# One factor and one shift for the first layer norm with modulation, the first head's scores earlier, gathers ahead of low parts, late weights in 8 KB rows

## The reference

```python
def ada_mod(c, w, b):
    m = jax.nn.silu(c) @ w + b
    shift, scale, gate = jnp.split(m, 3, axis=-1)
    return shift[:, None, :], 1.0 + scale[:, None, :], 1.0 + gate[:, None, :]

def layer_norm(x, g, b):
    xf = x.astype(jnp.float32)
    mu = jnp.mean(xf, axis=-1, keepdims=True)
    var = jnp.mean(jnp.square(xf - mu), axis=-1, keepdims=True)
    return ((xf - mu) * lax.rsqrt(var + LN_EPS)).astype(x.dtype) * g + b

def chunk(xc):                       # in peer_ffn, 128 tokens at a time
    q = (xc @ w_q).reshape(PEER_CHUNK, PEER_HEADS, 2, PEER_HALF)
    s = jnp.einsum('thpd,pnd->thpn', q, sub_keys).astype(jnp.float32)
    sv, si = lax.top_k(s, PEER_TOPK)
    ...
    top_s, pos = lax.top_k(cand_s, PEER_TOPK)
    idx = jnp.take_along_axis(cand_i, pos, axis=-1)
    g = jax.nn.softmax(top_s, axis=-1).astype(xc.dtype)
    act = jax.nn.gelu(jnp.einsum('td,thkd->thk', xc, u[idx]), approximate=False)
    return jnp.einsum('thk,thkd->td', g * act, v[idx])

def second_block(x, c, ...):
    for i in range(DEPTH):           # DEPTH = 2: short convolution, then differential attention
        shift, scale, gate = ada_mod(c, ada_w[i, 0], ada_b[i, 0])
        h = x * scale + shift
        f = mixer(h)
        x = layer_norm(DEEPNORM_ALPHA * x + gate * f, ln_g[i, 0], ln_b[i, 0])
        shift, scale, gate = ada_mod(c, ada_w[i, 1], ada_b[i, 1])
        h = x * scale + shift
        f = peer_ffn(h, peer_w_q[i], peer_sub_keys[i], peer_u[i], peer_v[i])
        x = layer_norm(DEEPNORM_ALPHA * x + gate * f, ln_g[i, 1], ln_b[i, 1])
    return x
```

## Time and profile before

| | |
|---|---|
| median of three runs | 2437.72 us (2437.59 to 2440.14) |
| the profiled execution | 2435.66 us, its span 2433.8 us |
| TensorE | busy 2106.9 us, 87% |
| VectorE | busy 1599.6 us, 66% |
| ScalarE | busy 1138.1 us, 47% |
| GpSimd | busy 639.6 us, 26% |
| DMA | 768.23 MB, mean 316 GB/s |
| the chain that ended last | PE 51%, DMA 25%, DVE 11%, ACT 8% |

### The profile page before, as it was taken

How to read it: one execution, slowest core, us unless ns; L and a number is a source line. 1 busy time by engine, 2 the same in 40 slices (tenths; PEclk the granted TensorE clock), 3 DMA queues, 4 the chain that set the end, 5 groups by cost and what they waited for, 6 DMA issues and landing times.

```text
span 2433.8 us, 28455 instructions
## 1 busy us (share of the span) xinstructions
PE 2106.9 (87%) x9804; PEld 1352.1 (56%) x9804; DVE 1599.6 (66%) x3701; ACT 1138.1 (47%) x2760; POOL 639.6 (26%) x624
## 2 busy tenths in 40 slices
PE   7769999998999987897777989987998898888776
PEld 7648999876999986452223434432444443323222
DVE  5685677664778777867667467556648656676753
ACT  4354543534653434435445375434447444444543
POOL 0010011000001004544443234243324334434441
PEclk8869999999999988999999999999999999999998
DMA  6234588541569745999999999999999999999995
GB/s 226 87 104 147 174 280 283 173 165 41 171 215 361 268 148 190 396 419 419 419 420 407 392 412 413 395 418 420 395 389 369 398 381 420 420 420 420 420 421 212
DMA packets 139013, 768.23 MB, mean 316 GB/s; under 512 B 15232, under 2 KB 18048, under 8 KB 73088
## 3 DMA queue, kind: packets, MB, share of 16 engines
q0 software_dynamic: 87552, 587.24, 59.6%
q1 hardware_dynamic: 50608, 177.81, 20.7%
q10 hardware_dynamic: 720, 1.51, 0.2%
HBM read 765.45 MB, written 1.05 MB: 315 GB/s over the span
## 4 chain that ended last, share of the span: by engine, by line
PE 51%; DMA 25%; DVE 11%; ACT 8%; issue 3%; POOL 1%; SPq 0%; ACTq 0%; POOLq 0%; DVEq 0%
DMA arena<-experts,arena 24%; PE bank L860 12%; PE bank L513 9%; PE bank L515 9%; PE bank L514 9%; PE bank L895 6%; DVE arena L2120 3%; DMA wring<-w_stream 2%; ACT L1335 1%; ACT arena L1340 1%; ACT arena L1339 1%; ACT arena L1157 1%; DVE arena L1678 1%; PE bank L613 1%; DVE wlo L1566 1%
## 5 line engine op out<-in xcount | busy, mean ns | idle before, releaser
L860 PE MATMUL bank<-arena 128*128 128x512 f32 x2048 | 983.2, 618 | 168.0 <-ACT arena L1340 167.6
L2120 DVE CUSTOM_DVE_ANT_0 arena<-arena 128x1024 f32<-128x1024 f32 x512 | 631.2, 1234 | 468.4 <-DMA arena<-experts,arena 467.4
L480 POOL DMA_INDIRECT arena<-experts,arena x512 | 560.0, 1094 | 862.6 <-PE bank L860 820.2
L860 PEld LDWEIGHTS bank<-arena 128*128 128x128 f32 x2048 | 374.1, 194 | 730.3 <-ACT arena L1340 374.8
L1566 DVE TENSOR_TENSOR wlo<-wring,whi 128x1024 fp32r<-128x1024 f32 x224 | 272.9, 1224 | 168.1 <-ACT whi L1083 167.3
L1083 ACT CAST whi<-wring 128x1024 fp32r<-128x1024 f32 x236 | 246.3, 1048 | 275.4 <-PE bank L515 274.0
L1335 ACT ACTIVATE arena<-arena 128x1 f32<-128x1 f32 x512 | 102.9, 201 | 472.3 <-DVE arena L2120 470.5
L1340 ACT ACTIVATE arena<-tab,arena 128x128 f32<-128x128 f32 x512 | 205.5, 401 | 16.7
L513 PE MATMUL bank<-hTh,whi 128*128 128x256 f32 (+1 forms) x640 | 192.3, 300 | 22.0 <-DVE hTl L1575 18.9
L466 POOL DMA_DIRECT2D arena<-ada_w x64 | 34.0, 531 | 664.7 <-DVE adaM L1613 646.5
L514 PE MATMUL bank<-hTl,whi 128*128 128x256 f32 (+1 forms) x640 | 187.3, 293 | 0.0
(11 more groups left out here) (304 smaller groups left out, 3039.1 us busy)
## 6 DMA issues: line engine op xcount, KB each, us to landing
wring<-w_stream SPq DMA_DIRECT2D x332, 512.0 KB, 4.7
arena<-ada_w POOLq DMA_DIRECT2D x64, 512.0 KB, 5.3
alibi<-ada_w POOLq DMA_DIRECT2D x32, 512.0 KB, 5.4
arena<-experts,arena POOLq DMA_INDIRECT x512, 14.2
xT<-xT_in SPq DMA_DIRECT2D x1, 1088.0 KB, 5.0
alibi<-alibi_in ACTq DMA_DIRECT2D x1, 1024.0 KB, 5.0
outT<-xT SPq DMA_DIRECT2D x2, 512.0 KB, 13.5
tab<-tab_in SPq DMA_DIRECT2D x1, 831.0 KB, 6.5
```

The lines of the kernel that those rows point to most:

```text
L480: pool.indirect_dma_start(g_ring[:, r], None, experts[n // (2 * PEER_HEADS)], bass.IndirectOffsetOnAxis(idx[:, s // SLOTS % 2, s % SLOTS:s ...
L860: last = mm(banks[2 * t + b][:, :], diag[:, r], g_ring[:, r, D + b * TILE_N:D + (b + 1) * TILE_N], start=s % SLOTS == 0, stop=s % SLOTS == ...
L2120: v.tensor_tensor_reduce(g_ring[:, r, 0:D], g_ring[:, r, 0:D], hrow[:, t], 1.0, 0.0, ALU.mult, ALU.add, act8[:, r:r + 1]).then_inc(dot_don ...
```

## The change

- The first layer norm with its modulation becomes one factor and one shift: `hf` is first the normalized value times g x (1 + scale); ScalarE adds the folded shift as the bias of the operation that makes `hTh`, VectorE's low part adds it too. The shift is added to `hf` itself afterwards (`hf_ready`), and the plain layer norm `x2` after that (`ln_done`). Three small products on VectorE before the residual make factor and shift.
- TensorE makes the first head's scores right behind its own two query chunks; scores of later heads stand between the two chunks of the next head. ScalarE copies in the same order.
- GpSimd does four low parts, waits for `ln_done`, and then issues gathers, with the low parts of tile 57 after slots 1, 2, 4 and 6; its wait for the turned rows stands at slot 3.
- The late 24 tiles come as two DMAs of 1 MB each, with rows of 8 KB; the host lays them out so that a half holds the rows of four steps of the contraction, and `half_tile` waits for and frees a half.
- The fifteen partial products leave the first attention: three go into the first MLP's start, twelve into the section of keys, values and queries of the second attention.

```diff
-        both_g, both_b = m(2, KC), m(2, KC)
+        both_g, both_b = m(3, KC), m(3, KC)
...
+        late_landed = [[sem(f"late_landed{s}_{h}") for h in range(2)] for s in range(2)]
...
+        def late_half(g, half):
+
+            return wring[:, g % 2, 2 * half:2 * half + 2].rearrange("p c k n -> p (c k n)")
...
-            for g in range(N_LOADS):
+            for g in range(G_QKV):
...
-                    sp.dma_start(wring[:, g % 2, c], w_stream[g if g < N_TILES else g - BESIDE, c]).then_inc(w_landed[g % 2][c], 16)
+                    sp.dma_start(wring[:, g % 2, c], w_stream[g, c]).then_inc(w_landed[g % 2][c], 16)
...
+            for g in range(G_QKV, N_LOADS):
+                tile = w_stream[g if g < N_TILES else g - BESIDE].rearrange("c p k n -> (c p k n)").rearrange(
+                    "(h p m) -> h p m", h=2, p=P)
+                for half in range(2):
+                    sp.wait_ge(lin_done, CPT * (g - 2) + 2 * half + 2)
+                    sp.dma_start(late_half(g, half), tile[half]).then_inc(late_landed[g % 2][half], 16)
...
             for c in range(CPT):
                 split_lo(G_PQ + 1, c)
-            split_lo(G_PQ + 2, 0)
-            pool.wait_ge(hrow_done, 4)
+            pool.wait_ge(ln_done, 8)
             for s in range(N_SLOTS):
+                if s == 3:
+                    pool.wait_ge(hrow_done, 4)
                 gather(s)
-                if s in (1, 3, 5):
-                    split_lo(G_PQ + 2, (s + 1) // 2)
+                if s in (1, 2, 4, 6):
+                    split_lo(G_PQ + 2, s // 2)
...
-                if half == 0:
-                    for c in range(CPT):
-                        pe.wait_ge(w_landed[g % 2][c], 16 * (g // 2 + 1))
-                for kc in range(4 * half, 4 * half + 4):
-                    last = mm(dst, lhs[:, kc], wring[:, g % 2, :, kc], start=kc == 0, stop=kc == KC - 1)
-                if half:
-                    last.then_inc(lin_done, CPT)
+                pe.wait_ge(late_landed[g % 2][half], 16 * ((g - G_QKV) // 2 + 1))
+                w = late_half(g, half)
+                for k in range(4):
+                    last = mm(dst, lhs[:, 4 * half + k], w[:, k * TILE_N:(k + 1) * TILE_N], start=half == 0 and k == 0,
+                              stop=half == 1 and k == 3)
+                last.then_inc(lin_done, CPT // 2)
...
+            def query_chunk(c):
+                if c >= 4:
+                    pe.wait_ge(pq_copied, c - 3)
+                chunk(G_PQ + c // CPT, c % CPT, banks[(2, 3, 6, 7)[c % 4]][:, 0:SEQ], pq_in, after(mod_split, 8) if c == 0 else None)
...
             for h in range(PEER_HEADS + 1):
                 if h < PEER_HEADS:
-
-                    for c in (2 * h, 2 * h + 1):
-                        g = G_PQ + c // CPT
-                        if c >= 4:
-                            pe.wait_ge(pq_copied, c - 3)
-                        chunk(g, c % CPT, banks[(2, 3, 6, 7)[c % 4]][:, 0:SEQ], pq_in, after(mod_split, 8) if c == 0 else None)
-                if h:
-
-                    y = h - 1
-                    if y == 0:
-                        pe.wait_ge(sk_landed, 16)
-                    pe.wait_ge(pq_copied, 2 * y + 2)
-                    if y >= 2:
-                        pe.wait_ge(sc_copied, y - 1)
-                    for t in range(2):
-                        for x in range(2):
-                            last = mm(banks[4 + y % 2][:, (2 * t + x) * P:(2 * t + x + 1) * P],
-                                      pqT[:, y % 2, x, t * P:(t + 1) * P], skT[:, x], start=True, stop=True)
-                    last.then_inc(sk_done, 1)
+                    query_chunk(2 * h)
...
+                if h >= 2:
+                    head_scores(h - 1)
+                if h < PEER_HEADS:
+                    query_chunk(2 * h + 1)
+                if h == 0:
+                    head_scores(0)
                 if 1 <= h < 3:
                     t = h - 1
                     for c in range(KC):
+                        if t == 0:
+                            pe.wait_ge(hf_ready, c + 1)
...
-            act.wait_ge(ln_done, 1)
+            act.wait_ge(mod_ready, 9)
...
-            hi_parts(hTh, hf, 0, SEQ, mod_ready, mod_hi, 8)
+            for kc in range(KC):
+                act.wait_ge(mod_ready, 8 + kc + 1)
+                af(hTh[:, kc, 0:SEQ], hf[:, kc], ACT.Identity, bias=both_b[:, 0, kc:kc + 1]).then_inc(mod_hi, 1)
...
-                    for x in range(2):
-                        c = 2 * h + x
-                        act.wait_ge(lin_done, CPT * G_PQ + c + 1)
-                        nc.scalar.copy(pqT[:, h % 2, x], banks[(2, 3, 6, 7)[c % 4]][:, 0:SEQ]).then_inc(pq_copied, 1)
-                        if c < 12:
-                            split_hi(G_PQ + c // CPT + 1, c % CPT)
-                if h:
-                    y = h - 1
-                    act.wait_ge(sk_done, y + 1)
-                    nc.scalar.copy(sc[:, y], banks[4 + y % 2][:, :].rearrange("p (t s n) -> p t s n", t=2, s=2)).then_inc(
-                        sc_copied, 1)
+                    query_copy(2 * h)
+                if h >= 2:
+                    copy_scores(h - 1)
+                if h < PEER_HEADS:
+                    query_copy(2 * h + 1)
+                if h == 0:
+                    copy_scores(0)
+                if 2 * h + 1 < 12:
+                    query_hi(2 * h + 1)
...
-                parts = ((0, 0, 0, 0, 1, 1, 1, 2, 2, 2, 2, 1, 1, 1, 1), (0, 0, 0, 0, 0, 0, 0, 0, 0, 0, 0))[layer]
...
-                    for _ in range(parts[n]):
-                        ada_part()
...
-                two(0, 1, True)
+                two(0, 1, True, 0 if layer else 3)
...
-                if x % 2:
-                    ada_part()
+                ada_part()
             for x in range(8):
                 split_lo(G_BQ + x // CPT + 1, x % CPT)
                 if x == 0:
                     head_root(0)
-                if x % 2:
-                    ada_part()
+                ada_part()
                 if x >= 2:
                     head_scale(x - 2)
             head_scale(6)
@@ -1902,12 +1934,14 @@
             split_lo(G_BV + 1, 1)
             for x in range(3):
                 head_scale(8 + x)
+                ada_part()
             decay_sums()
             split_lo(G_BV + 1, 2)
             split_lo(G_BV + 1, 3)
             for x in range(3, 6):
                 head_scale(8 + x)
                 ada_part()
+            ada_part()
...
+            def first_layer_norm():
...
+                for n in range(KC + 2):
+                    if n < KC:
+                        v.scalar_tensor_tensor(hf[:, n], xnT[:, n], both_g[:, 0, n:n + 1], rinv[:, 0, 0:SEQ], ALU.mult,
+                                               ALU.mult).then_inc(mod_ready, 1)
+                    if n >= 2:
+                        c = n - 2
+                        dve.wait_ge(mod_hi, 8 + c + 1)
+                        v.scalar_tensor_tensor(hTl[:, c, 0:SEQ], hf[:, c], both_b[:, 0, c:c + 1], hTh[:, c, 0:SEQ].bitcast(F32),
+                                               ALU.add, ALU.subtract).then_inc(mod_split, 1)
+                for c in range(KC):
+                    v.tensor_scalar(hf[:, c], hf[:, c], both_b[:, 0, c:c + 1], None, ALU.add).then_inc(hf_ready, 1)
                 scaled = []
-                for n in range(KC + 4):
+                for n in range(KC + 1):
                     if n < KC:
-                        mark(v.scalar_tensor_tensor(xnT[:, n], xnT[:, n], vcol("ln_g", 8 * i + n), rinv[:, 0, 0:SEQ], ALU.mult,
-                                                    ALU.mult))
+                        mark(v.scalar_tensor_tensor(xnT[:, n], xnT[:, n], vcol("ln_g", n), rinv[:, 0, 0:SEQ], ALU.mult, ALU.mult))
                         scaled.append(seq[0])
-                    if 1 <= n < KC + 1:
-                        c = n - 1
-                        dve.wait_ge(dve_seq, scaled[c])
-                        v.tensor_scalar(x2[:, c], xnT[:, c], vcol("ln_b", 8 * i + c), None, ALU.add).then_inc(ln_done, 1)
-                    if 2 <= n < KC + 2:
-                        dve.wait_ge(ln_done, n - 1)
-                        if dst is not None:
-                            modulate_chunk(i + 1, dst, n - 2)
-                    if n >= 4 and dst is not None:
-                        modulate_lo(i + 1, dst, n - 4)
+                    if n:
+                        dve.wait_ge(dve_seq, scaled[n - 1])
+                        v.tensor_scalar(x2[:, n - 1], xnT[:, n - 1], vcol("ln_b", n - 1), None, ALU.add).then_inc(ln_done, 1)
...
+            def norm_and_modulation(i):
+
+
+                g, b = vcol("ln_g", 8 * i, 8), vcol("ln_b", 8 * i, 8)
+                mark(v.tensor_tensor(both_g[:, i], g, adaM[:, i + 1, 8:16], ALU.mult))
+                link(v.tensor_tensor(both_b[:, i], b, adaM[:, i + 1, 8:16], ALU.mult))
+                link(v.tensor_tensor(both_b[:, i], both_b[:, i], adaM[:, i + 1, 0:8], ALU.add))
...
```

(5 more changed lines are left out.)

36 lines of the change are left out of this document (28 added, 8 removed).

## The result

The changed kernel takes 2413.22 us (median of six runs, 2412.54 to 2414.45), the kernel before beside it 2437.65 (2425.63 to 2440.14). The ratio is 0.9908 with a 95% interval of 0.9891 to 0.9925: 24.4 us less, where 18 were forecast (2419.8, range 2404 to 2434). The profiled execution has a span of 2412.6 us. The 24.4 us may hold some scatter of the kernel before: in 39 further executions, beside the experiments, its medians were 2432.13 to 2433.66, and the changed kernel measured once more took 2414.12. By these the gain is 18 to 20 us.

What follows compares the result with a forecast made beforehand. Bounds were read by stages: DMA engines full during gathers, TensorE and DMA limits close together in the mixers. Terms -6 - 4 - 8 = -18 from the profiled 2435.66, plus 2.1 to the median, gave 2419.8 us, range 2404 to 2434.

Steps and rivals of the forecast that it cites:

- Term 1: First attention: fifteen partial products leave it, their new places cost 0; -6 us, from -8 to 0.
- Term 2: Way from the first layer norm to the first gather: an earlier selection starts gathers sooner; -4 us, from -8 to +0.5.
- Three or four such meetings: Before the selection: VectorE's tail operations stretched beside GpSimd's low parts, so the tail ends at 940 to 947 us.
- a start 4 us sooner moves the end by 4: From the first gather on: DMA engines were full from 960 us, so an earlier start counts in full, 4 us.
- Term 3: Late 24 weight tiles in 8 KB rows, two DMAs each: DMA time freed, partly gained; -8 us, from -20 to 0.
- 2 x 0.8: Two late tiles ahead of the mixers: the gain in us counted for them from wider rows.
- I take some 20 us of DMA time as freed: Late 24 tiles: 8 KB rows instead of 4 KB save some 20 us of the DMA engines' time.
- rate of 349 GB/s: First mixer: weights' rate worked out with gathers at 420 GB/s, taken as showing that 4 KB rows run slower.
- TensorE's wait for late weights is small, so 0: Late tiles: waiting for and freeing a half alone was counted as a gain of 0 us.
- the 5.1 MB that it moved less: Second mixer against first: 12 us less DMA work in the same 300 us, so less DMA time became idleness.
- pushes the gathers aside: Rival, mixers: weights take half the DMA engines instead of a third, gathers delayed, 37 us slower, 2464.7 us; chance 0.06.
- Idleness: Rival: DMA time freed by wide rows is idle anyway, so that gain is 0, 2427.7 us; chance 0.24.

Runs made afterwards that it cites:

- parts_back: The changed kernel with the fifteen partial products back in the first attention and none in the new places: 2420.09 us.
- norm_old: The changed kernel with the first layer norm and modulation as before, in place of the one factor and shift: 2417.33 us.
- scores_late: The changed kernel with each head's scores again behind the next head's two query chunks, ScalarE copying in that order: 2410.95 us.
- rows4k: The changed kernel with each late half as two DMAs with rows of 4 KB, halves still waited for and freed singly: 2414.18 us.

## Why the prediction was right, and where it was wrong

**Term 1** (-6) held: 4.3 us between the two profiles, 6.6 against parts_back, 4.0 in the times of one group. The new places cost nothing that can be told, as forecast.

**Term 2** (-4) was mis-sized: 5.8. The selection began 8.9 us sooner against the reciprocal, where 8 had been worked out for the scores alone: they were ready sooner than that (their copy ends at 934), and VectorE's tail, which ended at 935.2, was what the selection followed. Wrong was who waits for whom: "Three or four such meetings put the end of the tail at 940 to 947". In the tail VectorE kept its pace and GpSimd was made to wait. The lock cost 3.9 us in the selection itself, on two operations. The Trainium skill, "SBUF — State Buffer", section "Who interferes with whom", has it that issue order decides who blocks; the 7.23 us on GpSimd and the 2.23 on VectorE agree with that, and the prediction had allowed for one side alone. How much of the 5.8 is time isn't settled: the step "a start 4 us sooner moves the end by 4" holds for norm_old (2.8 at the gather and 3.2 in time) and not for scores_late (2.3 and none).

**Term 3** (-8) was mis-sized and stood on a wrong step: 12.7 us came from gather 128 to gather 368, the two mixers, and 1.3 ahead of them. The 1.3 is what "2 x 0.8" had for the two tiles there, and the rows show it (about 1.5 us). "I take some 20 us of DMA time as freed" was 9, and rows4k shows that in the mixers those 9 are not time. The rate of 349 GB/s, worked out for weights in the mix, is the pace of a queue that shares, not the price of a row. The Trainium skill, "DMA: Bandwidth & Descriptors", section "iDMA fabric — 4 AXI ports for 8 engines, asymmetric across TPBs", has 408.7 GB/s for a stream alone with 4 KiB rows, by which the prediction's estimate was 3 us. The 9 us lie nearer to that than to the 20, and no run here times the late rows alone. The step that failed most is "TensorE's wait for late weights is small, so 0". The waits were 5.05 us in two places; the clock behind the longer one took another 3.15. So the second mixer, to which I gave 2 us, gained 9.1, 6.1 of it at that one place and 2.2 where TensorE waited 5.34 us for VectorE (the last 0.8 was not traced): its 300 us were not the bound of TensorE's order, they held stalls and matmuls at the lower clock. Nor were the 5.1 MB that it moved less a sign of idleness: 4.2 MB of them are two weight tiles fewer in that stretch (20.97 MB in the weights' queue for 25.17).

**The rivals.** The one that pushes the gathers aside was right in its first half at most: with the rows and DMA sizes alone changed they land 1.3 us later in one stretch, and no later over both mixers. The price was not paid; that eight of them stand in line may be why, and no run varies that. "Idleness" was right about the DMA time freed in the mixers and wrong about the term, since the same edit also took away waits.

So the range held because each of three terms was right in sign, not because the third was understood. For the third that is luck: its number came from a price of rows that the runs do not bear out, and the gain from waits that had been put at 0.

## What to carry to other kernels

Look at the few places where the engine that sets the pace waits for a load, even where they sum to 5 us: compare the time from the place coming free to its use (15.1 us here) with the time from there to the last byte while other queues run (17.3, and 13.9 in the median with the wide rows). When a few us are missing, any one of an earlier release, a wait for less, or a larger part of the DMA engines can close most of the gap, and the next one adds little; so test them together as well as one by one. A stream's share divided by its bytes, taken while it shares the engines, is no price for the shape of its rows.

## What the runs showed of the hardware

- A wait of 2.77 us on TensorE was followed by a granted clock of 0.52 from 1780 to 1785 us and 3.15 us of loss on eight matmuls, more than the wait itself. One of 2.28 us at 1364.09 was not: the clock stayed at 1.00 from 1364 to 1369 us.
- VectorE's products with two inputs, one every 0.66 us with sums between them, held one low part on GpSimd for 7.23 us instead of 2.37, over several VectorE instructions until the last of them was done. A low part that runs already holds a cast of 128 x 32 on VectorE for 2.27 us (0.18 alone), and an integer operation on 128 x 16 for 2.42 (0.17 alone).
- Beside gathers, a 2 MB tile as two DMAs of 8 KB rows was there in 13.9 us (median of 22, from the first issue to the last landing), and as four DMAs of 4 KB rows in 18.3, with all else the same. Which of the two, the rows or the size of a DMA, does it is not separated.
